# Eight input norms of a two-block transformer kernel: where the squares are kept and summed, one weight split, two rotary rotations

## The chip, the cores and the metric

One core of one Trainium2 chip runs the whole program. The metric is the device time in microseconds. Five engines matter: TensorE (PE in the profile; PEld is its weight load), VectorE (DVE), ScalarE (ACT), GpSimd (POOL) and SyncE (SP), which starts the weight transfers.

## The reference, cut to what matters

The program computes two blocks of depth 2 on 512 tokens of width 1024, in float32. The change touches the second one, and the norm on the border to it:

```
h = layer_norm(DEEPNORM_ALPHA * h + ff, ln2_g[l], ln2_b[l])      # end of the first block

for i in range(2):                                                # second block
    h = h + 0.5 * rms_norm(swiglu(rms_norm(h, g[0]), ...), g[1])
    hn = rms_norm(h, g[2])
    y = dilated_mixer(hn, ...) if i == 0 else window_gqa_mixer(hn, ...)   # mixer A, mixer B
    h = h + rms_norm(y, g[3])
    h = h + 0.5 * rms_norm(swiglu(rms_norm(h, g[4]), ...), g[5])
    e = p[i] @ ple_proj[i]
    gate = sigmoid(rms_norm(h, g[6]) @ ple_gate[i])
    h = h + rms_norm(e * gate, g[7])
```

`rms_norm(x, g)` is `x * rsqrt(mean(x*x)) * g`. Both mixers rotate the first 16 of the 64 features of each head of q and k (`apply_rope`): a swapped copy of the features is multiplied by a sine table and added to the features times a cosine table.

## The kernel before, in words

Activations lie transposed: 1024 features are 8 chunks (`DC`) of 128 partitions with 512 tokens along the free dimension. Every large product is made in three matmuls of 128 x 128 x 512 per pair of weight block and chunk (`piece`, L877 to L879): float32 is split into a high and a low part, and high*high, high*low, low*high are added. A unit of weights is 128 x 1024, eight such blocks. SyncE fetches units in order into a ring of four (`raw`), plus one unit set apart at the start of a section. ScalarE makes the high part `wh` (L1581) and VectorE the low part `wl` (L2058), in the order written in their streams; a ring place becomes free when TensorE has finished the unit that held it. TensorE waits for a unit's low part (`split_done`) before it uses the unit. All five streams are written out in one fixed order; the mixers' order comes from the generators `plan_a` and `plan_b`.

An RMS norm ahead of a product is not applied to the input. The product starts on the input times the gain, and the factor `rs_in` is multiplied in when VectorE takes a finished tile out of its bank. There are eight such places: ahead of ffn2 four times (once on the border to the second block, where the input comes out of `layer_norm`; three times behind `residual`), ahead of mixer A, ahead of mixer B, and ahead of the gate product twice. At each of them:

- VectorE's `residual` runs over the chunks k: the low part of the input `low_part(k)` (L2127), the sum `add(k+1)` (L2150), the part `part(k+2)` (L2145), and from k = 1 on `add_square(k)` (L2136), which adds the square of chunk k to `acc`. ScalarE's `pre_chunk(k)` makes the high part of the input (L1638) and then the square (`square`, L1603) into `sq[k % 2]`; from the third chunk on it first waits until VectorE has read that buffer.
- TensorE takes the chunks as they come: `first_tiles` works on three output tiles abreast (L921, L922, L928), nine matmuls for a chunk, and on a fourth tile that trails two chunks behind (ahead of the gate: four chunks behind), three matmuls for a chunk.
- When the three tiles are finished, and three pieces (gate: five pieces) of the fourth are still to be made, TensorE waits for the squares' sum and multiplies it by a matrix of 1/1024 (`pre_sum`, L1048). ScalarE then splits the unit behind the first four (`begin`), makes `rs_in` from the sum (L1595, L1596), and VectorE, which has split the same unit, uses `rs_in`: directly on tiles (L2197, L2763), or, ahead of a mixer, on the cosine and sine tables (`trig`, L2581, L2582).

In the mixers a tile of q or k is then rotated. VectorE shuffles (L2590) and multiplies by the cosine (L2591), which frees the bank, and GpSimd's `rope` multiplies the shuffled copy by the sine (L810) and adds (L811). `roped` of tile k waits until the rotation of two tiles earlier is over, since the shuffled copies alternate between two buffers. Splits of weight units stand between the tiles in VectorE's stream. Mixer B's first tiles are k0, v0, q0, q1 and k1; TensorE makes its first attention scores after two blocks of the fifth tile, and ahead of them it runs 20 matmuls of a constant (`stay_awake_in_next(20)`, L973), each of which the profile counts as two.

Ahead of the gate, TensorE still makes the embedding products while the chunks arrive. Five units are needed for them and the first three gate tiles: the third gate tile's unit is split by VectorE in `emb_splits` after chunk 2, the fourth tile's after chunk 4. In the stream of TensorE `first_tiles(GATED, before=before)` puts seven constant matmuls ahead of the third tile.

Of the kernel before, what the change touches and what calls it, by code (L numbers as in the profile page):

```python
# [391 lines left out]
def build(nc, stream, x_t, p_t, small, vecs, tab1, tab_a, tab_b, consts, out):  # L392
    n_units = stream.shape[0]
    with ExitStack() as ctx:
# [178 lines left out]

        SQ_HOMES = {2: prod[0], 3: prod[1], 5: tmp[0], 6: tmp[1], 7: sq[1]}
# [81 lines left out]
        def _(pool):  # L656
# [167 lines left out]
            def ropes_b():  # L824
                c.start(banks_mixer)
                for stage, k in plan_b():
                    if stage == "unit" and k < len(B_TILES):
                        c.next_tile()
                        if B_TILES[k][0] != "v":
                            rope(b_home(k)[:, :], tbb[:, B_SIN:B_SIN + S])  # L830
                    elif stage == "part":
                        c.next_tile()
# [38 lines left out]
        def _(pe):  # L871
# [16 lines left out]
            def unit(dst, src, chunks, start, stop, ready=None):  # L888

                pe.wait_ge(split_done, c.at("unit") + 1)  # L890
                for j, kc in enumerate(chunks):
                    if ready is not None:
                        c.wait(ready)
                    mm = piece(dst, c.n.get("unit", 0), kc % 8 * P, src, kc, start and j == 0,
                               stop and j == len(chunks) - 1)
                mm.then_inc(unit_done, 1)
                c.tick("unit")

            def tile(src, spread=(range(8),), ready=None):

                dst = free_tile()
                for n, chunks in enumerate(spread):
                    unit(dst, src, chunks, n == 0, n == len(spread) - 1, ready=ready)
# [9 lines left out]
            def abreast(u, t, kc, width, summed=True):  # L913
# [18 lines left out]
                if kc == 7 and summed:  # L932
                    pre_sum()

            def first_tiles(order, summed=True, before=None):
# [3 lines left out]
                for t, kc in order:  # L939
# [5 lines left out]
                    if t < width:  # L945
                        abreast(u, t, kc, width, summed)
                        continue
# [274 lines left out]
            def dense_n(layer, n, order):  # L1222
# [11 lines left out]
                if n < len(order):  # L1234
                    abreast(unit0[0], m, j, 2 if layer else 1, summed=False)
                    return
# [34 lines left out]
            for layer in range(DEPTH):  # L1271
# [57 lines left out]
                for half in range(2):  # L1329
                    if half == 0:  # L1330
                        first_tiles(BY_THREE, summed=False)
# [21 lines left out]
            def dense(n, n_tiles, part, o, outs0):  # L1353
# [150 lines left out]
            def mixer_b():  # L1504
                unit0[0] = c.n["unit"]
                c.start(banks_mixer)
                for stage, k in plan_b():
# [15 lines left out]
            for layer in range(DEPTH):  # L1523
# [44 lines left out]
        def _(act):  # L1568
# [67 lines left out]
            def pre_chunk(g, k, ready):  # L1636
# [18 lines left out]
            def rms_pre(g, then=None):  # L1655

                for k in range(DC):
                    pre_chunk(g, k, h_ready)
# [49 lines left out]
            for layer in range(DEPTH):  # L1708
# [142 lines left out]
                for m in range(DC):  # L1851
# [9 lines left out]
                    if m == 4:  # L1861
                        for k in range(5):
# [5 lines left out]
                           None if layer == 0 else lambda k: pre_chunk(V_RMS, k, affine))  # L1868
# [180 lines left out]
        def _(dve):  # L2049
# [27 lines left out]
            def layer_norm(g, to_x, wide=False):  # L2077
# [22 lines left out]
                for k in range(DC):  # L2100
# [14 lines left out]
                    if not to_x:  # L2115
                        add_square(k)
                        if k + 3 < DC:
                            centre(k + 3)
                if wide:
# [20 lines left out]
            def residual(g, pre, then=None):  # L2140
# [14 lines left out]
                for k in range(DC):  # L2155
# [5 lines left out]
                    add_square(k)  # L2161
# [431 lines left out]

            def part_of(m, last):
# [108 lines left out]
            def mixer_b():  # L2703
                trig(tbb[:, B_COS:B_COS + S], tbb[:, B_SIN:B_SIN + S], rs_in[:, :])
                c.start(banks_mixer)
                for stage, k in plan_b():
                    if stage == "unit":
                        unit_over()
                        if k < len(B_TILES):
                            src = bank[c.peek()][:, :]  # L2710
                            if B_TILES[k][0] == "v":
                                free(dve.tensor_tensor(bvs[:, :], src, rs_in[:, :], ALU.mult))
                            else:
# [19 lines left out]
            for layer in range(DEPTH):  # L2733
# [12 lines left out]
                def emb_splits(k):  # L2746
                    if k in (2, 4):
# [206 lines left out]
```

## Time and profile before

| | us |
|---|---|
| median of 3 runs | 3413.58 (3413.32 to 3414.89) |
| the profiled execution's own time | 3413.37 |
| its span, first to last instruction | 3411.5 |
| TensorE busy | 3339.1 (98%) |
| VectorE busy | 1836.1 (54%) |
| ScalarE busy | 1241.5 (36%) |
| GpSimd busy | 342.4 (10%) |

The profile shows one execution. Its own time is 1.9 us more than its span, and 0.2 us below the median. Busy time of TensorE counts the constant matmuls as work. The granted TensorE clock was 0.997 on the mean.

### The profile page before, as it was taken

How to read it: one execution, taken by the hardware profiler on the slowest of the kernel's cores; microseconds unless marked ns; L12 is line 12 of the kernel's file. 1: busy time of each engine (PE TensorE's matmuls, PEld its weight loads, DVE VectorE, ACT ScalarE, POOL GpSimd, SP SyncE). 2: the span in 40 equal slices, each digit the busy share in tenths (PEclk: the TensorE clock that was granted, in tenths of full speed). 3: DMA queues.
4: the chain of work that ended last, by engine and by line, in shares of the span. 5: the costliest groups of instructions: out<-in, count | busy, mean ns of one | idle time of the engine just before them, and what ended most of it. 6: DMA issues, size and time to landing. Idle time of an engine off the chain costs nothing.

```text
span 3411.5 us, 43291 instructions
## 1 busy us (share of the span) xinstructions
PE 3339.1 (98%) x16950; PEld 2661.6 (78%) x16950; DVE 1836.1 (54%) x2932; ACT 1241.5 (36%) x1878; POOL 342.4 (10%) x244
## 2 busy tenths in 40 slices
PE   9999999999999999999999999999999999999998
PEld 6767888776688887888777778887788876788886
DVE  5766334567753446443566664435644357654436
ACT  3354223424442324322333343324422235532324
POOL 0310000213100020000132200000000012100001
PEclk9999999999999999999999999999999999999999
DMA  4102232321122222223322122232222321132232
GB/s 163 62 32 73 94 99 98 124 69 44 56 81 99 96 95 87 93 97 105 113 69 71 66 81 98 95 103 98 87 92 98 105 95 43 58 104 93 99 106 79
DMA packets 81434, 300.40 MB, mean 88 GB/s; under 512 B 9040, under 2 KB 9040, under 8 KB 80640
## 3 DMA queue, kind: packets, MB, share of 16 engines
q1 hardware_dynamic: 78624, 284.20, 24.9%
q0 software_dynamic: 1568, 11.98, 0.9%
q8 instruction: 106, 1.74, 0.2%
q10 hardware_dynamic: 1088, 2.10, 0.2%
q14 instruction: 48, 0.39, 0.0%
HBM read 296.14 MB, written 2.10 MB: 87 GB/s over the span
## 4 chain that ended last, share of the span: by engine, by line
PE 88%; DVE 6%; ACT 3%; issue 1%; POOL 1%; DMA 1%; ACTq 0%; DVEq 0%; POOLq 0%
PE bank L877 25%; PE bank L879 25%; PE bank L878 25%; PE bank L921 2%; PE bank L928 2%; PE bank L922 2%; DVE wl L2058 1%; ACT sc L1742 1%; PE bank L1431 1%; PE bank L1443 1%; PE bank L1191 1%; PE bank L1172 1%; ACT wh L1581 1%; PE bank L1486 1%; PE bank L1130 1%
## 5 line engine op out<-in xcount | busy, mean ns | idle before, releaser
L877 PE MATMUL bank<-x,wh 128*128 128x512 f32 x2632 | 1053.1, 400 | 16.9 <-DVE h L2502 5.7
L879 PE MATMUL bank<-x,wl 128*128 128x512 f32 x2632 | 1027.3, 390 | 0.0
L878 PE MATMUL bank<-x,wh 128*128 128x512 f32 x2632 | 1026.3, 390 | 0.0
L1581 ACT ACTIVATE wh<-raw 128x1024 fp32r<-128x1024 f32 x528 | 558.1, 1058 | 1155.8 <-PE bank L879 1086.5
L2058 DVE TENSOR_TENSOR wl<-raw,wh 128x1024 fp32r<-128x1024 f32 x528 | 677.9, 1285 | 548.5 <-ACT wh L1581 547.3
L877 PEld LDWEIGHTS bank<-x,wh 128*128 128x128 f32 x2632 | 494.8, 188 | 138.2 <-issue 30.2
L879 PEld LDWEIGHTS bank<-x,wl 128*128 128x128 f32 x2632 | 494.5, 188 | 105.0
L878 PEld LDWEIGHTS bank<-x,wh 128*128 128x128 f32 x2632 | 495.3, 188 | 98.0 <-issue 3.4
L877 PE MATMUL bank<-mid,wh 128*128 128x512 f32 x1216 | 474.9, 391 | 0.5 <-DVE wl L2058 0.5
L878 PE MATMUL bank<-mid,wh 128*128 128x512 f32 x1216 | 473.1, 389 | 0.0
L879 PE MATMUL bank<-mid,wl 128*128 128x512 f32 x1216 | 473.1, 389 | 0.0
L877 PEld LDWEIGHTS bank<-mid,wh 128*128 128x128 f32 x1216 | 228.2, 188 | 49.6 <-DVE wl L2058 1.4
L878 PEld LDWEIGHTS bank<-mid,wh 128*128 128x128 f32 x1216 | 228.2, 188 | 48.1 <-issue 1.0
L879 PEld LDWEIGHTS bank<-mid,wl 128*128 128x128 f32 x1216 | 228.2, 188 | 47.6
L2197 DVE TENSOR_TENSOR prod<-bank,rs_in 128x512 f32<-128x512 f32 x88 | 60.7, 690 | 232.6 <-PE bank L879 232.6
L2074 DVE TENSOR_TENSOR mid<-prod,mid 128x512 f32 (+1 forms) x152 | 104.8, 689 | 88.4 <-ACT mid L1882 85.6
L680 POOL TENSOR_TENSOR acc<-sq,sq 128x512 f32<-128x512 f32 x8 | 11.2, 1398 | 1291.3 <-ACT sq L1687 1291.3
L2514 DVE TENSOR_TENSOR prod<-tmp,bank 128x512 f32<-128x512 f32 x64 | 43.9, 687 | 142.7 <-ACT tmp L1832 142.7
L1882 ACT ACTIVATE mid<-prod 128x512 f32 (+1 forms) x88 | 55.6, 632 | 174.7 <-DVE prod L2562 174.7
L1832 ACT ACTIVATE tmp<-bank 128x512 f32<-128x512 f32 x64 | 38.1, 595 | 178.4 <-PE bank L879 178.4
L921 PE MATMUL bank<-x,wh 128*128 128x512 f32 x200 | 80.1, 401 | 14.7 <-ACT x L1704 6.8
L2197 DVE TENSOR_TENSOR tmp<-bank,rs_in 128x512 f32<-128x512 f32 x88 | 60.8, 691 | 59.6 <-PE bank L879 58.4
(342 smaller groups left out, 3348.1 us busy)
## 6 DMA issues: line engine op xcount, KB each, us to landing
raw<-stream SPq DMA_DIRECT2D x528, 512.0 KB, 3.3
raw_apart<-stream SPq DMA_DIRECT2D x10, 512.0 KB, 3.6
sm<-small POOLq DMA_DIRECT2D x2, 2144.0 KB, 10.2
tb<-tab POOLq DMA_DIRECT2D x2, 1728.0 KB, 14.4
h<-x_t ACTq DMA_DIRECT2D x4, 512.0 KB, 7.1
out_t<-h SPq DMA_DIRECT2D x8, 256.0 KB, 2.1
tba<-tab_a POOLq DMA_DIRECT2D x1, 1152.0 KB, 9.2
pf<-p_t POOLq DMA_DIRECT2D x2, 512.0 KB, 5.2
```

What stands on the lines that cost most here:

```text
L877: pe.matmul(dst, hi, src[:, kc, 0, :], start=start, stop=False)
L878: pe.matmul(dst, hi, src[:, kc, 1, :], start=False, stop=False)
L879: return pe.matmul(dst, lo, src[:, kc, 0, :], start=False, stop=stop)
L921: pe.matmul(dst, hi, x[:, kc, 0, :], start=kc == 0, stop=False)
L922: pe.matmul(dst, lo, x[:, kc, 0, :], start=False, stop=False)
L928: mm = pe.matmul(dst, hi, x[:, kc, 1, :], start=False, stop=kc == 7)
L1581: act.activation(high_of(n)[:, :], raw_of(n)[:, :], ACT.Copy).then_inc(hi_done, 1)
L1882: act.activation(mid[:, i * 2 + k, 0, :], prod[k][:, :], ACT.Copy).then_inc(mid_hi, 1)
L2058: dve.tensor_tensor(low_of(n)[:, :], raw_of(n)[:, :], high_of(n)[:, :].bitcast(F32), ALU.subtract).then_inc(split_done, 1)
L2074: dve.tensor_tensor(dst, src, hi.bitcast(F32), ALU.subtract).then_inc(done, 1)
L2197: free(dve.tensor_tensor(dst, bank[c.peek()][:, :], rs_in[:, :], ALU.mult))
L2514: free(dve.tensor_tensor(prod[k % 2][:, :], tmp[k % 2][:, :], b[:, :], ALU.mult))
```

## The change

- ScalarE writes the squares of a norm's input to eight homes of their own, the chunks of `y` (used up by then), and behind the layer norm to `sq`, `tmp` and the upper four chunks of `y`. It waits for no reader.
- VectorE adds nothing after chunks 1 to 3, one square each after chunks 4, 5 and 6, and four after chunk 7. Behind the layer norm, the additions also stand after `centre` and not before it.
- TensorE's `pre_sum` moves behind the remaining pieces of the fourth tile: in the mixers and at the gate directly behind `first_tiles`, in ffn2 two further pieces later, inside the fifth tile.
- At the gate, the third gate tile's unit is split after chunk 1 (was 2), and the seven constant matmuls ahead of that tile are gone.
- In mixer B, the rotations of k0 and q0 are made on VectorE alone (`roped_whole`: shuffle, cosine product, sine product, sum), and the constant matmuls ahead of the first scores are 13 (were 20).

```diff
+        LN_HOMES = [sq[0][:, :], sq[1][:, :], tmp[0][:, :], tmp[1][:, :]] + [y[:, k, :] for k in range(4, DC)]
@@ GpSimd, ropes_b
-                        if B_TILES[k][0] != "v":
+                        if B_TILES[k][0] != "v" and k < 3:
+                            c.tick("rope")
+                        elif B_TILES[k][0] != "v":
                             rope(b_home(k)[:, :], tbb[:, B_SIN:B_SIN + S])
@@ TensorE
+            def unit(dst, src, chunks, start, stop, ready=None, sums=None):
                 pe.wait_ge(split_done, c.at("unit") + 1)
                 for j, kc in enumerate(chunks):
+                    if j == sums:
+                        pre_sum()
...
@@ abreast
-                if kc == 7 and summed:
-                    pre_sum()
@@ ffn2
                 first_tiles(BY_THREE)
                 for k in range(4):
-                    tile(x)
+                    tile(x, sums=2 if k == 0 else None)
@@ dense (mixers)
+                if n == len(BY_THREE):
+                    pre_sum()
@@ mixer_b
-                            stay_awake_in_next(20)
+                            stay_awake_in_next(13)
@@ gate
-                def before(t):
-                    if t == 2:
-                        stay_awake(7)
-                    pe.wait_ge(emb_read, 8 * layer + 3 + t)
-
-                first_tiles(GATED, before=before)
+                first_tiles(GATED, before=lambda t: pe.wait_ge(emb_read, 8 * layer + 3 + t))
+                pre_sum()
@@ ScalarE, pre_chunk
-                square(k)
+                act.activation(home[:, :], h[:, k, :], ACT.Square).then_inc(sq_made, 1)
+                c.tick("sqm")
@@ VectorE
-            def add_square(k):
-                if k:
-                    both = 2 if k == 1 else 1
+            def add_squares(k, homes):
+                for m in {4: [1], 5: [2], 6: [3], 7: [4, 5, 6, 7]}.get(k, []):
+                    both = 2 if m == 1 else 1
                     c.wait(sq_made, both)
-                    dve.tensor_tensor(acc[:, :], sq[0][:, :] if k == 1 else acc[:, :], sq[k % 2][:, :],
+                    dve.tensor_tensor(acc[:, :], homes[0] if m == 1 else acc[:, :], homes[m],
                                       ALU.add).then_inc(sq_used, both)
                     c.wait(sq_used, both)
...
+            def roped_whole(dst, src):
+                k = c.n.get("roped", 0)
+                dve.wait_ge(rotated, k)
+                rt = prod[k % 2][:, :]
+                link(dve.stream_shuffle(rt, src, SWAP))
+                free(dve.tensor_tensor(dst, src, tbb[:, B_COS:B_COS + S], ALU.mult))
+                link(dve.tensor_tensor(rt, rt, tbb[:, B_SIN:B_SIN + S], ALU.mult))
+                settled()
+                dve.tensor_tensor(dst, dst, rt, ALU.add).then_inc(rotated, 1)
+                c.tick("roped")
...
                 def emb_splits(k):
-                    if k in (2, 4):
+                    if k in (1, 4):
                         c.wait(unit_done)
                         split()
```

## Rows read from the trace of the kernel before

**Rows 1.** The page, part 1: engine, busy us, share of the span, instructions.
```profile
PE 3339.1 (98%) x16950; PEld 2661.6 (78%) x16950; DVE 1836.1 (54%) x2932; ACT 1241.5 (36%) x1878; POOL 342.4 (10%) x244
```

**Rows 2.** Waits of TensorE: us in total, times, longest us.
```profile
PE bank L921 <- ACT x L1638: 4.6, 6, 1.1
PE bank L1486 <- DVE scb L2645: 2.9, 4, 2.1
```

**Rows 3.** Groups by line, TensorE: busy us, mean ns | idle us before them.
```profile
L1048 PE MATMUL bank<-acc,ones 128*128 128x512 f32 x16 | 8.2, 590 | 0.0
```

**Rows 4.** Timeline of VectorE, first gate: start us, us, what, [idle before <-releaser].
```profile
2351.56 0.69 DVE L2136 TENSOR_TENSOR acc<-sq,sq 128x512 f32<-128x512 f32 x1
...
2354.93 1.23 DVE L2058 TENSOR_TENSOR wl<-raw,wh 128x1024 fp32r<-128x1024 f32 x1
...
2361.38 1.23 DVE L2058 TENSOR_TENSOR wl<-raw,wh 128x1024 fp32r<-128x1024 f32 x1
```

**Rows 5.** Timeline of ScalarE, first gate.
```profile
2350.49 1.05 ACT L1581 ACTIVATE wh<-raw 128x1024 fp32r<-128x1024 f32 x1
...
2352.82 1.06 ACT L2008 ACTIVATE emb<-bank 128x512 f32<-128x512 f32 x2
```

**Rows 6.** Timeline of TensorE, first gate, ahead of the third tile.
```profile
2354.10 1.72 PE L973 MATMUL bank<-ident,ones 128*128 128x128 f32 x14
2356.30 0.47 PE L921 MATMUL bank<-x,wh 128*128 128x512 f32 x1 [0.48 <-DVE wl L2058]
```

**Rows 7.** Timeline of TensorE, first gate, ahead of the fifth tile.
```profile
2379.56 0.47 PE L877 MATMUL bank<-x,wh 128*128 128x512 f32 x1 [1.25 <-DVE wl L2058]
```

**Rows 8.** Timeline of TensorE, third ffn2: the norm's matmul, starts of tiles five and six.
```profile
2429.48 1.02 PE L1048 MATMUL bank<-acc,ones 128*128 128x512 f32 x2
...
2432.43 0.39 PE L877 MATMUL bank<-x,wh 128*128 128x512 f32 x1
...
2437.87 0.39 PE L877 MATMUL bank<-x,wh 128*128 128x512 f32 x1
```

**Rows 9.** Timeline of VectorE, third ffn2: the split ahead of the fifth tile.
```profile
2430.41 1.22 DVE L2058 TENSOR_TENSOR wl<-raw,wh 128x1024 fp32r<-128x1024 f32 x1 [2.07 <-ACT wh L1581]
```

**Rows 10.** Timeline of TensorE, mixer A: the norm's matmul, starts of tiles six and seven.
```profile
1686.30 1.02 PE L1048 MATMUL bank<-acc,ones 128*128 128x512 f32 x2
...
1694.81 0.47 PE L877 MATMUL bank<-x,wh 128*128 128x512 f32 x1
...
1702.29 0.47 PE L877 MATMUL bank<-x,wh 128*128 128x512 f32 x1 [1.75 <-DVE wl L2058]
```

**Rows 11.** Timeline of VectorE, mixer A: cosine table, splits for tiles six and seven.
```profile
1688.74 1.05 DVE L2581 TENSOR_TENSOR tba<-tba,rs_in 128x512 f32<-128x512 f32 x1 [0.28 <-ACT rs_in L1596]
...
1693.29 1.38 DVE L2058 TENSOR_TENSOR wl<-raw,wh 128x1024 fp32r<-128x1024 f32 x1
...
1699.81 2.33 DVE L2058 TENSOR_TENSOR wl<-raw,wh 128x1024 fp32r<-128x1024 f32 x1
```

**Rows 12.** Timeline of TensorE, mixer B: constant matmuls, first scores, first transposes of probabilities.
```profile
2802.49 4.62 PE L973 MATMUL bank<-ident,ones 128*128 128x128 f32 x40
2807.96 0.70 PE L1474 MATMUL bank<-bk,bq 64*128 64x256 f32 x4 [0.84 <-POOL bq L811]
...
2817.44 0.33 PE L1486 MATMUL bank<-ident,scb 128*128 128x128 f32 x1 [2.10 <-DVE scb L2645]
```

**Rows 13.** Timeline of VectorE, mixer B: k0's shuffle, a split, the first scores' masking.
```profile
2799.24 0.74 DVE L2590 STREAM_SHUFFLE prod<-bank 128x512 f32<-128x512 f32 x1
...
2801.06 2.02 DVE L2058 TENSOR_TENSOR wl<-raw,wh 128x1024 fp32r<-128x1024 f32 x1
...
2808.77 0.38 DVE L2695 COPY scb<-sink 128x2 f32<-128x2 f32 x1 [2.00 <-PE bank L1474]
```

**Rows 14.** Windows: stretch, its us, busy us of each engine (instructions), PEclk, DMA share, GB/s.
```profile
279.70:283.11 3.41, 1.57 (x7) 0.99 (x6) 3.38 (x4) 1.41 (x2) 1.59 (x2) 1.00 0.08 34
283.11:286.52 3.41, 3.41 (x10) 2.61 (x9) 2.73 (x4) 1.26 (x2) 2.14 (x2) 0.50 0.01 2
```

More of the change, by code:

```diff
@@ L886, in free_tile @@
                 return bank[b][:, :]
-            def unit(dst, src, chunks, start, stop, ready=None):
+            def unit(dst, src, chunks, start, stop, ready=None, sums=None):
                 pe.wait_ge(split_done, c.at("unit") + 1)
                 for j, kc in enumerate(chunks):
+                    if j == sums:
+                        pre_sum()
                     if ready is not None:
@@ L897, in unit, with tile @@
                 c.tick("unit")
-            def tile(src, spread=(range(8),), ready=None):
+            def tile(src, spread=(range(8),), ready=None, sums=None):
                 dst = free_tile()
                 for n, chunks in enumerate(spread):
-                    unit(dst, src, chunks, n == 0, n == len(spread) - 1, ready=ready)
+                    unit(dst, src, chunks, n == 0, n == len(spread) - 1, ready=ready, sums=sums)
             def tiles_of(n, src, spread=(range(8),), ready=None):
@@ L911, in tiles_of, with abreast @@
                         tile(src, spread)
-            def abreast(u, t, kc, width, summed=True):
+            def abreast(u, t, kc, width):
                 if t == 0:
@@ L931, in abreast, with first_tiles @@
                         c.tick("unit")
-                if kc == 7 and summed:
-                    pre_sum()
-            def first_tiles(order, summed=True, before=None):
+            def first_tiles(order, before=None):
                 u = c.n["unit"]
@@ L945, in first_tiles @@
                     if t < width:
-                        abreast(u, t, kc, width, summed)
+                        abreast(u, t, kc, width)
                         continue
@@ L1234, in dense_n @@
                 if n < len(order):
-                    abreast(unit0[0], m, j, 2 if layer else 1, summed=False)
+                    abreast(unit0[0], m, j, 2 if layer else 1)
                     return
@@ L1330, in _ @@
                     if half == 0:
-                        first_tiles(BY_THREE, summed=False)
+                        first_tiles(BY_THREE)
                         for k in range(4):
@@ L1634, in begin, with pre_chunk @@
                 c.tick("begun")
-            def pre_chunk(g, k, ready):
+            def pre_chunk(g, k, ready, home):
                 c.wait(ready)
                 act.activation(x[:, k, 0, :], h[:, k, :], ACT.Copy, scale=vec[:, g + k:g + k + 1]).then_inc(x_hi, 1)
-                square(k)
+                act.activation(home[:, :], h[:, k, :], ACT.Square).then_inc(sq_made, 1)
+                c.tick("sqm")
             def unit_over():
@@ L1657, in rms_pre @@
                 for k in range(DC):
-                    pre_chunk(g, k, h_ready)
+                    pre_chunk(g, k, h_ready, y[:, k, :])
                     if then is not None:
@@ L1867, in _ @@
                 layer_norm(V_LN + 32 * layer + 16, V_LN + 32 * layer + 24, layer == 0,
-                           None if layer == 0 else lambda k: pre_chunk(V_RMS, k, affine))
+                           None if layer == 0 else lambda k: pre_chunk(V_RMS, k, affine, LN_HOMES[k]))
             def ffn2(embed=False):
@@ L2115, in layer_norm @@
                     if not to_x:
-                        add_square(k)
                         if k + 3 < DC:
                             centre(k + 3)
+                        add_squares(k, LN_HOMES)
                 if wide:
@@ L2160, in residual @@
                         part(k + 2)
-                    add_square(k)
+                    add_squares(k, [y[:, m, :] for m in range(DC)])
                     if then is not None:
@@ L2712, in mixer_b @@
                                 free(dve.tensor_tensor(bvs[:, :], src, rs_in[:, :], ALU.mult))
+                            elif k < 3:
+                                roped_whole(b_home(k)[:, :], src)
                             else:
```

## The prediction

> **What bounds the kernel now.** I read the page first: TensorE is busy for 98% of the span, the next engine for 54% [rows 1]. So nothing that only makes VectorE or ScalarE shorter can be seen in the time; what counts is where TensorE stands idle or runs constants. The second view was the list of TensorE's waits. It is short. One entry that lies where this change works is mixer B's probabilities (L1486); of the chunks of a norm's input it names the high part (L1638), six times in all, which is the start of the first chunk, and never the low part L2127 [rows 2]. The third was the group of the norm's own matmul: 8 calls, counted as 16, with 0.0 us of idle time before them [rows 3]. The squares' sum is never late today. That is the main thing for the reader to see: the change takes work off the path to a matmul that nobody waits for, and then puts that matmul later. What hangs behind it (`rs_in`, the tables, the first tiles) comes later too, so the question is who has slack there. For that I went through the timelines of the eight norms.
>
> The pace of TensorE: 24 matmuls from 2432.43 to 2437.87 [rows 8], 0.227 us each, so a chunk of nine takes 2.04 us and, with the trailing tile's three, 2.72 us. One L2136 addition is 0.69 us [rows 4].
>
> **Squares in homes of their own, additions at the end.** Three additions (2.0 us of VectorE) go from chunks 1 to 3 to the end, where four stand in a row: about 2.9 us at 0.69 plus 0.03 for the wait between them. In today's third ffn2 the last one ends 2 us before VectorE's next split, which waits for ScalarE [rows 9]; with three more at the end and the earlier chunks shorter by as much, they still end before that split starts. I take 0. It would be a gain if TensorE were waiting for chunks behind the first, which the list of waits doesn't show [rows 2]; idle times too short for it, one matmul's 0.2 us at each of eight norms, are the lower bound, -1.6. If the additions delay the split by as much as one of them, it costs +0.7 at each of six norms, 4 us, the upper bound. The value is nearest the first row, since the wait of 2.07 us ahead of the split [rows 9] is larger than what moves.
>
> **The norm's matmul moved behind three pieces, ffn2.** In the third ffn2 it starts at 2429.48 and the fifth tile at 2432.43 [rows 8]: nine matmuls are 2.04 us of that, the norm's matmul costs 0.91. Without it the fifth tile would start at 2431.52, but its unit's low part ends at 2430.41 + 1.22 = 2431.63 [rows 9], and TensorE resumes 0.15 us after such an end (the split of 1699.81 + 2.33 and the start at 1702.29 [rows 10, 11]): 2431.78. So 0.26 us of idle time appears that the norm's matmul covers today. The 0.91 is then paid inside the tile. Four such places: +1.0 us. `rs_in` is 3.4 us later there; the first bank that needs it is wanted by the sixth tile at 2437.87, and is free by about 2436. That cover holds, with 1.8 us to spare.
>
> **The same in mixer A.** Here the cover is missing. The norm's matmul goes from 1686.30 [rows 10] to 1688.34 + 0.26 = 1688.60, and all that VectorE does behind it moves by 2.3 us: the tables at 1688.74, two rotations, and only then the low part for the sixth tile, 1693.29 to 1694.67 [rows 11]. TensorE starts that tile at 1694.81 today, 0.14 us behind the split: no slack. It will start at 1697.1, after 2.1 us idle. The seventh tile waits 1.75 us today for the split at 1699.81 [rows 10, 11], in the same chain of VectorE and GpSimd; it moves by 2.3 us too. Those are one delay and not two: +2.3 us. Lower end 0 (if VectorE's order left slack that I don't see), upper end 2.3 plus one more wait of GpSimd's addition, about 1.3.
>
> **The same in mixer B, with two whole rotations on VectorE and seven fewer constants.** Twenty constants take 4.62 us, counted x40 [rows 12], so thirteen take 3.0. Today TensorE waits 0.84 us more behind them for GpSimd's second rotation, until 2807.96. In the new order k0 starts at 2799.24 + 2.30 = 2801.54 [rows 13]. A whole rotation occupies VectorE for a shuffle with its wait 0.79, cosine 0.61, sine with its wait 0.73 and sum 0.61: 2.74 us, against 1.24 today. These two operations are not in VectorE's rows; I price them as additions of the same shape [rows 4], bounds 0.6 and 1.3 each. Then v0 0.60, a split and q0: the split takes 2.02 us today, beside GpSimd's two operations [rows 13], and I take 1.2, as others do [rows 4], since GpSimd has nothing to do there any more. q0 is rotated at 2808.85, the scores start at 2808.9: +0.95. TensorE idles 2.8 us ahead of them, so the missing constants bring nothing by themselves.
>
> The Trainium skill, SBUF — State Buffer, section "Who interferes with whom", says that a VectorE instruction with two SBUF inputs and a GpSimd instruction that reads SBUF exclude each other for their whole length. The 2.02 us agrees with it. Without the rule, with 2.02 kept, the sum would be 0.8 us longer.
>
> After q0 come q1 (1.24) and the split behind it (1.2), and only then the masking of the first scores: 2811.2 in place of 2808.77, where VectorE today idles 2.00 us for TensorE [rows 13]. That idle time is used up. Behind it the order is as before, less a wait of 0.5 us for ScalarE: the transposes that start at 2817.44 [rows 12] start at 2819.3, +1.85 us, and TensorE idles 3.1 us ahead of them instead of 2.10. Bounds: +0.9 (only the scores' delay is kept) and +3.5 (sine and sum at 1.3 each, and the split contended).
>
> **The gate's third split.** The third tile waits for the low part made from 2354.93 to 2356.16 [rows 4]; until then TensorE runs seven constants for 1.72 us and idles 0.48 [rows 6]. The high part has been there since 2351.54 [rows 5], so behind chunk 1, where the addition of 2351.56 falls away, VectorE can split from 2351.6 to 2352.8. The bank is read out by the first of two copies from 2352.82 [rows 5], in the new order slightly earlier: free at 2353.4. TensorE can go on at 2354.10, where the constants stood: -2.20 us at each of two gates, -4.4. Chunk 2's low part then comes at 2353.5 and is wanted after 2357. The fourth tile's split is at 2361.38 today [rows 4] and will be near 2361; the tile is wanted at 2363.5. The norm's matmul moves behind 15 matmuls but is still ahead of the wait of 1.25 us for the fifth tile [rows 7], which hangs on a transfer started by the finished first tile and doesn't change. Bounds: -4.8 and 0.
>
> **Sum.** -4.4 + 1.0 + 2.3 + 1.85 = +0.8. From the profiled execution's 3413.37 (span 3411.5, 1.9 around it) that is 3414.1; the median shown is 0.2 higher, so 3414.4. What a measurement of this kernel can tell from no change is about 0.2%, 6.8 us: this is no change.
>
> **Rivals.**
>
> 1. *The clock gives way in the mixers (slower).* With 1.57 us of work in 3.41 us, 1.84 idle in one piece, the granted clock was 0.50 in the stretch that followed, the lower of its two levels, 1.2 GHz [rows 14]; behind 1.75 [rows 10] and 2.10 us idle [rows 12] it stayed up. I forecast idle times of 2.1 and 2.0 (mixer A), 2.8 and 3.1 us (mixer B). A stretch of 3.41 us at half clock is 1.7 us of work lost. Behind the first of each pair that is hidden in the second wait; behind the second nothing hides it: 1.7 in each mixer, 3417.8. [...] For it: the missing seven constants lengthen the idle piece. Against it: 2.10 us did nothing. 0.25.
> 2. *The mixers absorb the delay (faster).* If the tables were ready sooner than I derive, or the low parts are reordered in effect by ScalarE's earlier squares, the gates' gain stands alone: -4.4 + 1.0, 3410.2. Against it is the split that is waited for to 0.14 us today [rows 10, 11]. 0.22.
> 3. *The gate's change doesn't do what it says.* If the bank or the high part is late behind chunk 1, TensorE idles where it ran constants and only the costs are left: +0.8 + 4.4, 3418.8. The high part ends 0.05 us before VectorE wants it [rows 4, 5], but the tile is wanted 1.3 us after that. 0.07.
>
> The forecast has 0.46.
>
> **How the numbers follow.** All four cases lie within 0.2% of the time before. Rival 2 with the chunks' whole 1.6 us is 3408.6, the end of what I can add up on the fast side; rivals 1 and 3 together would be 3422. The range 3409.3 to 3418.9 leaves about one in ten out at either end together. Faster than 0.2% (under 3406.8) needs more idle time than these places have: 0.04. Slower than 0.2% (over 3420.4) needs rivals 1 and 3 together, or the upper ends of both mixers with rival 1: 0.07. No change: 0.89.
>
> **What would show it.** Gate: no L973 ahead of the third tile, which follows the second within 0.3 us; if L973's place is filled by an idle time, rival 3. ffn2: an idle time of about 0.1 to 0.3 us ahead of the fifth tile, L1048 six matmuls later. Mixer A: idle times of about 2 us ahead of both the sixth and the seventh tile, released by wl L2058; one of them missing would make the step wrong. Mixer B: about 2.8 us ahead of the first scores, released by a VectorE sum, about 3 us ahead of the first transposes. PEclk at 0.50 in either mixer would be rival 1. Additions that end later than ScalarE's high part behind the first tiles, or an idle time before L1048, would upset the first step.

## The result, and the profile after

| us | before | after |
|---|---|---|
| median of 11 runs beside each other | 3413.60 (3411.93 to 3415.61) | 3422.32 (3420.82 to 3424.64) |
| ratio of the times | | 1.0026 [1.0018, 1.0033] |
| the profiled execution, own time / span | 3413.37 / 3411.5 | 3423.08 / 3421.2 |

The change costs 8.7 us, 0.26%. The forecast was 3414.4, no change; the time lies above the forecast's range (3409.3 to 3418.9), and above the 0.2% that the prediction took as the border between slower and no change.

The page after, part 1, answers to [rows 1]: TensorE's busy share is the same and 42 instructions (the constants) are gone.

```profile
PE 3340.6 (98%) x16908; PEld 2658.1 (78%) x16908; DVE 1840.2 (54%) x2936; ACT 1240.0 (36%) x1878; POOL 336.4 (10%) x240
```

The waits of TensorE after (us in total, times, longest us), beside [rows 2]. L880 is the L877 of before.

```profile
PE bank L880 <- DVE wl L2059: 13.1, 10, 2.0
...
PE bank L926 <- ACT x L1638: 4.6, 6, 1.1
...
PE bank L1479 <- DVE bq L2605: 2.6, 1, 2.6
...
PE bank L1491 <- DVE scb L2659: 2.3, 4, 1.5
```

and the one row of before that answers to the first:

```profile
PE bank L877 <- DVE wl L2058: 5.9, 6, 1.8
```

Waits for a weight unit's low part have gone from six to ten and from 5.9 to 13.1 us. Five are new: one of 1.56 us in each ffn2, and one of 2.01 us in mixer A. One of 1.25 us at the start of the program is put down to another releaser in this list. The first experiment takes the four of ffn2 away again. The chunks' entry (L1638) is unchanged to the tenth, and the idle time before the norm's matmul is 0.1 us at all eight places together, where it was 0.0 (groups by line, as [rows 3]):

```profile
L1051 PE MATMUL bank<-acc,ones 128*128 128x512 f32 x16 | 8.3, 602 | 0.1
```

TensorE runs the same 12720 weight matmuls in the same order in both kernels. So one can lay the two timelines beside each other, matmul by matmul, and read how far each part of the program has slipped. That table, in us, is the backbone of what follows. It compares one profiled execution with one other:

| part | forecast | profiled pair |
|---|---|---|
| first block, not touched | 0 | +1.04 |
| ffn2, four times | +0.26 each | +2.27, +2.28, +2.28, +2.28 |
| mixer A | +2.3 | +2.31 |
| mixer B | +1.85 | +1.88 |
| gate, twice | -2.2 each | -2.29, -2.29 |
| sum | +0.8 | +9.8 |

The first block's +1.04 is, on balance, one more stretch of 3.4 us at half clock, near 930 us in this execution; the medians differ by 8.7. What the forecast missed stands in one row of the table, the ffn2's: 8.1 us. The row of mixer B needs care. Three more kernels below have the same mixer B, and the profile of each shows its own number, by where and for how long the granted clock fell: +1.9, +3.1 and +4.5.

**Third ffn2.** TensorE after, tile five, the norm's matmul, tile six. Beside it [rows 8].

```profile
2437.25 0.47 PE L880 MATMUL bank<-x,wh 128*128 128x512 f32 x1
...
2438.72 1.02 PE L1051 MATMUL bank<-acc,ones 128*128 128x512 f32 x2
...
2445.42 0.47 PE L880 MATMUL bank<-x,wh 128*128 128x512 f32 x1 [1.56 <-DVE wl L2059]
```

In [rows 8] the sixth tile has no idle time before it. Now it has 1.56 us, and not for a bank: for `wl`, the low part of its own weights. VectorE and ScalarE after, in the same place:

```profile
2435.88 1.23 DVE L2059 TENSOR_TENSOR wl<-raw,wh 128x1024 fp32r<-128x1024 f32 x1 [1.36 <-ACT wh L1581]
2441.16 0.69 DVE L2199 TENSOR_TENSOR tmp<-bank,rs_in 128x512 f32<-128x512 f32 x1 [4.05 <-ACT rs_in L1596]
2441.76 0.68 DVE L2199 TENSOR_TENSOR prod<-bank,rs_in 128x512 f32<-128x512 f32 x1
2444.05 1.23 DVE L2059 TENSOR_TENSOR wl<-raw,wh 128x1024 fp32r<-128x1024 f32 x1 [1.60 <-ACT wh L1581]
```

```profile
2439.77 0.69 ACT L1595 ACTIVATE rs_in<-bank,eps 128x512 f32<-128x512 f32 x1 [4.02 <-PE bank L1051]
2440.49 0.63 ACT L1596 ACTIVATE rs_in<-rs_in 128x512 f32<-128x512 f32 x1
2441.14 1.28 ACT L1878 ACT_TABLE_LOAD   x1
2442.43 0.63 ACT L1878 ACTIVATE tmp<-tmp 128x512 f32<-128x512 f32 x1
2442.97 1.04 ACT L1581 ACTIVATE wh<-raw 128x1024 fp32r<-128x1024 f32 x1
```

Before, the last two of these steps were (ScalarE, then VectorE):

```profile
2433.74 1.04 ACT L1581 ACTIVATE wh<-raw 128x1024 fp32r<-128x1024 f32 x1
```

```profile
2434.82 1.23 DVE L2058 TENSOR_TENSOR wl<-raw,wh 128x1024 fp32r<-128x1024 f32 x1 [1.60 <-ACT wh L1581]
```

Read ScalarE from top to bottom: the logarithm of the mean square, `rs_in` made from it, a table load, the activation of the scaled tile, and only then the high part of the sixth tile's unit. That unit needs nothing of the norm. ScalarE stands 4.02 us and VectorE 4.05 us in front of `rs_in` with its split behind them in the same streams. Before, the low part ended at 2434.82 + 1.23 = 2436.05, 1.82 us ahead of the tile, of which 0.15 is TensorE's resuming: 1.67 us of slack. In the kernel after, it ends at 2445.28, which is 9.23 later; the fifth tile starts 4.82 later; relative to it the split has moved by 4.41. The fifth tile itself is longer by the norm's matmul and a slower restart, 1.0. So 4.41 - 1.67 - 1.0 = 1.74 us are missing, and the start at 2445.42 comes 1.95 behind the last matmul at 2443.47 (one takes 0.23), 1.72 idle. That the two agree checks the bookkeeping only, since both come from this trace. From rows of before alone, `rs_in` 3.4 us later (the prediction's figure) less 1.67 us of slack is 1.7 us, an estimate that could have been made ahead. The fifth tile's own 0.26 (2437.25 against 2436.76 + 0.23) is exactly as forecast. The rest of the 2.28 is the first matmul behind each idle time, 0.31 in place of 0.23, and a little ahead of the seventh tile.

**Mixer A** is as forecast: idle times ahead of the sixth and the seventh tile, both released by the split, while [rows 10] has only the second.

```profile
1700.45 0.47 PE L880 MATMUL bank<-x,wh 128*128 128x512 f32 x1 [2.01 <-DVE wl L2059]
...
1707.90 0.47 PE L880 MATMUL bank<-x,wh 128*128 128x512 f32 x1 [1.75 <-DVE wl L2059]
```

**Mixer B.** VectorE after: the whole rotation of k0 and the split behind it, beside [rows 13]; then TensorE beside [rows 12].

```profile
2809.36 0.74 DVE L2601 STREAM_SHUFFLE prod<-bank 128x512 f32<-128x512 f32 x1
2810.14 0.69 DVE L2602 TENSOR_TENSOR bk<-bank,tbb 128x512 f32<-128x512 f32 x1
2810.74 0.68 DVE L2603 TENSOR_TENSOR prod<-prod,tbb 128x512 f32<-128x512 f32 x1
2811.46 0.69 DVE L2605 TENSOR_TENSOR bk<-bk,prod 128x512 f32<-128x512 f32 x1
...
2812.67 1.21 DVE L2059 TENSOR_TENSOR wl<-raw,wh 128x1024 fp32r<-128x1024 f32 x1
```

```profile
2816.63 0.49 PE L1479 MATMUL bank<-bk,bq 64*128 64x256 f32 x2 [2.58 <-DVE bq L2605]
...
2827.09 0.44 PE L1491 MATMUL bank<-ident,scb 128*128 128x128 f32 x2 [1.50 <-DVE scb L2659]
```

The rotation occupies VectorE for 2.71 us (priced 2.74), and the split takes 1.21 us, where it took 2.02 beside GpSimd's two operations. The second wait is 1.50 us and not the forecast 3.1, yet the sum is right. The windows (columns as in [rows 14]) say why:

```profile
2814.84:2818.25 3.41, 1.62 (x8) 1.15 (x9) 3.38 (x7) 0.00 (x0) 0.30 (x1) 1.00 0.01 2
2818.25:2821.66 3.41, 3.41 (x11) 1.72 (x10) 3.34 (x9) 1.38 (x2) 3.08 (x2) 0.50 0.35 108
```

Behind the idle time ahead of the scores the granted clock was 0.50 for one stretch, its lower level, 1.2 GHz; TensorE did its work there slower, arrived at the second wait later by that much, and found less of it. Where the clock held until then, in the run with three pieces below, the second wait was 3.07 us.

**Gate.** TensorE after, the end of the second tile's block and the start of the third's: nothing between them, where [rows 6] has 1.72 us of constants and 0.48 idle.

```profile
2361.71 0.39 PE L927 MATMUL bank<-x,wl 128*128 128x512 f32 x1
2361.93 0.39 PE L926 MATMUL bank<-x,wh 128*128 128x512 f32 x1
```

### The profile page after: what moved, and what is told of

Same layout as the page of the kernel before. It is cut to its first block, busy times and chain, and to the rows that moved or that the text cites. A ratio compares the mean times of both kernels' runs of the same rounds, so it can differ in the third digit from the quotient of the medians.

```text
span 3421.2 us, 43216 instructions
## 1 busy us (share of the span) xinstructions
PE 3340.6 (98%) x16908; PEld 2658.1 (78%) x16908; DVE 1840.2 (54%) x2936; ACT 1240.0 (36%) x1878; POOL 336.4 (10%) x240
## 3 DMA queue, kind: packets, MB, share of 16 engines
q8 instruction: 106, 1.74, 0.2%
## 4 chain that ended last, share of the span: by engine, by line
PE 88%; DVE 6%; ACT 3%; issue 2%; POOL 1%; DMA 0%; DVEq 0%; POOLq 0%; ACTq 0%
PE bank L880 25%; PE bank L882 25%; PE bank L881 25%; PE bank L926 2%; PE bank L927 2%; PE bank L933 2%; DVE wl L2059 1%; PE bank L1436 1%; ACT sc L1743 1%; PE bank L1448 1%; ACT wh L1581 1%; PE bank L1194 1%; PE bank L1175 1%; PE bank L1491 1%; PE bank L1133 1%
## 5 line engine op out<-in xcount | busy, mean ns | idle before, releaser
L880 PE MATMUL bank<-x,wh 128*128 128x512 f32 x2632 | 1053.4, 400 | 24.5 <-DVE wl L2059 12.6
L880 PEld LDWEIGHTS bank<-x,wh 128*128 128x128 f32 x2632 | 494.7, 188 | 149.5 <-issue 44.0
L880 PE MATMUL bank<-mid,wh 128*128 128x512 f32 x1216 | 474.9, 391 | 0.5 <-DVE wl L2059 0.5
L880 PEld LDWEIGHTS bank<-mid,wh 128*128 128x128 f32 x1216 | 228.3, 188 | 49.7 <-DVE wl L2059 1.3
```

Of the source, the lines that this page charges most:

```text
L880: pe.matmul(dst, hi, src[:, kc, 0, :], start=start, stop=False)
```

## The experiments

Theory 1 says that the ffn2's cost is the sixth tile's split behind a later `rs_in`. Theory 2 says that it is the additions at the end of the chunks, or the squares' new homes. Runs of one group share their runs of the kernel before, whose median was 3413.68 beside the first four, 3413.66 beside the others. Each kernel has 11 runs and one profile. Shifts are those of TensorE's weight matmuls against the profile of before. The ten kernels differ from before by less than 0.2%, so the places are told apart by the shifts.

**The norm's matmul of ffn2 back behind the three tiles abreast** (all else as after).

```diff
@@ first_tiles
+                        if summed and t == width - 1 and kc == 7:
+                            pre_sum()
@@ ffn2
-                first_tiles(BY_THREE)
+                first_tiles(BY_THREE, summed=True)
                 for k in range(4):
-                    tile(x, sums=2 if k == 0 else None)
+                    tile(x)
```

> The changed kernel with one part undone: in the four ffn2 the norm's matmul stands again directly behind the three tiles abreast; homes, additions at the end, gate, mixers stay changed. Theory 1 (queue): in ffn2 the low part of the sixth tile's unit stands behind rs_in in the streams of ScalarE and VectorE; rs_in 3.4 us later uses up the 1.8 us in which that low part was early, and TensorE idles 1.6 us ahead of the sixth tile and 0.1 ahead of the fifth, 2.28 us in each ffn2 by the shift of its matmuls. It expects -9.1 us against the changed kernel: 3413.2, no idle time ahead of the sixth tile. Theory 2 (additions): the four additions in a row, or the squares in y, hold up VectorE: 3422 stays, or TensorE now idles ahead of the norm's matmul (the last addition ends 0.4 us before that place).

Measured: 3413.39 (3411.05 to 3416.52), 0.9998 [0.9989, 1.0007]. The shift in every ffn2 is 0.0, with homes and late additions in place, and the waits for low parts fall back from 13.1 to 6.4:

```profile
PE bank L880 <- DVE wl L2061: 6.4, 6, 2.0
```

The 9 us are the place of this one matmul. Theory 2 falls. Mixer B, which is that of the kernel after, shows +3.1 here: the clock was 0.50 for 6.83 us behind a wait of 2.59 us ahead of the scores.

**The same in ffn2 and in the mixers.**

```diff
+                    if m == 2 and kc == 7:
+                        pre_sum()
-                if n == len(BY_THREE):
-                    pre_sum()
```

> As the kernel before this one, and the norm's matmul is also back at its old place in both mixers (the gates keep the new one). Theory 1: the mixers' shifts of +2.3 us (A) and +1.9 us (B) go as well: 3409.0, the sixth tile of mixer A starts without a wait of 2 us. Theory 2: if the whole rotations on VectorE are what costs in mixer B, only mixer A's 2.3 goes: 3411.

Measured: 3410.17 (3408.22 to 3412.21), 0.9988 [0.9979, 0.9997]. Mixer A's shift goes from +2.3 to 0.0, the gates keep -2.34 and -2.29. Mixer B still has +2.25, although its first transposes start 0.45 us earlier in the mixer than before: from 2814.69 on the granted clock was 0.50 for 6.83 us. The time lies between the 3409.0 and the 3411 expected and can't choose between the theories; the trace says that the delay of the transposes came from the moved matmul and that the clock then took the time anyway.

**The gate's change alone**, on the kernel before.

```diff
-                def before(t):
-                    if t == 2:
-                        stay_awake(7)
-                    pe.wait_ge(emb_read, 8 * layer + 3 + t)
-                first_tiles(GATED, before=before)
+                first_tiles(GATED, before=lambda t: pe.wait_ge(emb_read, 8 * layer + 3 + t))
@@ VectorE
-                    if k in (2, 4):
+                    if k in (1, 4):
```

> The kernel before with the gate's change alone: third tile's unit split behind chunk 1, the seven constant matmuls gone. Theory 1: -2.3 us at each of two gates, 3409.1 against 3413.6, the third tile starts directly behind the second. Rival: the gain needs the additions out of VectorE's way (here one of 0.69 us stands ahead of the split), and TensorE idles 0 to 0.5 us ahead of the third tile: 3410.

Measured: 3410.40 (3409.05 to 3411.55), 0.9990 [0.9981, 0.9999]. At the third tile the shifts are -2.29 and -2.30; with the wait for the fifth tile, which changes a little, they are -2.49 and -2.15. The median, 3.3 us faster, is nearer to the rival's 3410 than to 3409.1, but the rival's idle time isn't there. The third tile starts at the very time at which the constants did in [rows 6]:

```profile
2354.10 0.39 PE L921 MATMUL bank<-x,wh 128*128 128x512 f32 x1
```

**The two whole rotations and the 13 constants alone**, on the kernel before: the change's `roped_whole`, GpSimd's `ropes_b` for k < 3, and 20 to 13 in `stay_awake_in_next`.

```diff
+                            elif k < 3:
+                                roped_whole(b_home(k)[:, :], src)
-                            stay_awake_in_next(20)
+                            stay_awake_in_next(13)
```

> The kernel before with the two whole rotations on VectorE and 13 constant matmuls alone; the norm's matmul at its old place. Theory 1 (the delay of mixer B comes from the moved norm's matmul): the first scores start about 1.3 us earlier than before, the masking behind them at the same time, the first transposes 0 to 0.5 us earlier: 3413.2, no difference that can be measured. Rival (the rotations load VectorE too much): the first transposes come 1.5 to 2 us later: 3415.4.

Measured: 3415.64 (3411.90 to 3416.88), 1.0004 [0.9995, 1.0013]. TensorE after the constants:

```profile
2806.22 0.49 PE L1476 MATMUL bank<-bk,bq 64*128 64x256 f32 x2 [0.97 <-DVE bq L2605]
...
2816.66 0.47 PE L1488 MATMUL bank<-ident,scb 128*128 128x128 f32 x1 [3.08 <-DVE scb L2659]
```

and its windows:

```profile
2815.57:2818.98 3.41, 2.32 (x8) 2.03 (x9) 3.06 (x15) 2.48 (x8) 0.29 (x1) 0.50 0.01 2
2818.98:2822.40 3.42, 3.42 (x16) 1.76 (x14) 0.00 (x0) 0.62 (x3) 0.00 (x0) 0.50 0.00 0
```

The scores come at 2806.22 and not 2807.96 [rows 12], the transposes at 2816.66 and not 2817.44, so the rotations do what they are for. But TensorE reaches the transposes earlier still, idles 3.08 us in place of 2.10, and then works at half clock: the mixer ends 2.1 us later. The expectation of no difference missed the clock. The rival's 3415.4 came, but not by its mechanism, since the transposes aren't late. The interval of the times includes no change.

**The norm's matmul three pieces later in ffn2** (after has five): two pieces, 1.36 us, less delay.

```diff
-                    tile(x, sums=2 if k == 0 else None)
+                    tile(x, sums=0 if k == 0 else None)
```

> The changed kernel, the norm's matmul in ffn2 three pieces later than of old instead of five (ahead of the fifth tile's first block). Theory 1 (queue): rs_in comes 2.3 us later than of old in place of 3.65, the sixth tile's low part 0.5 to 0.7 us too late in place of 1.56 plus what the fifth tile loses; 0.6 to 0.9 us in each ffn2 instead of 2.28: about 3416.2. A rival in which the place itself costs (a float32 matmul between pieces, the weights' loads around it) expects no change from 3422.3.

Measured: 3416.85 (3414.66 to 3419.93), 1.0007 [0.9998, 1.0017]; shifts in ffn2 +0.84, +0.85, +0.81, +0.84. From the 1.74 missing above, 1.36 less leaves 0.38; with the fifth tile's 0.26 and two slow restarts that is 0.8. The price follows the delay beyond the slack, not the move as such. Mixer B, again that of the kernel after, shows +4.5: the clock held behind the first wait, and fell for 6.83 us behind the second.

```profile
2821.44 0.69 PE L1491 MATMUL bank<-ident,scb 128*128 128x128 f32 x2 [3.07 <-DVE scb L2659]
```

```profile
2820.52:2823.93 3.41, 2.49 (x8) 2.21 (x9) 2.92 (x13) 2.65 (x8) 0.12 (x1) 0.50 0.01 2
```

**The norm's matmul where after has it, the sixth tile's unit split ahead of `rs_in`** in ffn2.

```diff
@@ ScalarE
-            def pre_rstd():
+            def pre_rstd(early=0):
                 begin()
+                split(early)
@@ VectorE
-            def begin():
+            def begin(early=0):
                 c.wait(unit_done)
-                split()
+                split(1 + early)
@@ both, ffn2: no split behind the second tile
-                two(0, AFTER_NORM)
+                two(0, (0, 0, 0))
```

> The changed kernel with the norm's matmul left at its new place, but in ffn2 the sixth tile's unit is split ahead of rs_in on ScalarE and VectorE (its transfer has landed 1.8 us before the norm's matmul ends) and not behind the second tile. Theory 1 (the low part stands behind rs_in in the streams): the wait of 1.56 us ahead of the sixth tile goes, 0.3 to 0.7 us are left in each ffn2: 3415.5. Rival (late rs_in itself, by way of banks that are not free): the wait stays, released by a tile's reader and not by wl: 3422.3.

Measured: 3414.51 (3413.31 to 3417.24), 1.0003 [0.9994, 1.0012]; shifts +0.39, +0.39, +0.32, +0.39. VectorE, first ffn2, splits and then takes `rs_in`:

```profile
1324.44 1.23 DVE L2060 TENSOR_TENSOR wl<-raw,wh 128x1024 fp32r<-128x1024 f32 x1 [2.23 <-ACT wh L1581]
...
1326.26 0.69 DVE L2200 TENSOR_TENSOR tmp<-bank,rs_in 128x512 f32<-128x512 f32 x1 [0.60 <-ACT rs_in L1596]
```

This is the decisive run: counted from the start of this ffn2, VectorE takes the first tile with `rs_in` at the same time as in the kernel after, to 0.01 us, so that the banks come free no earlier, and 1.9 of the 2.28 us are gone. The bank was never the matter. What is left is nearly the forecast 0.26.

**Homes and additions alone**: after, with `pre_sum` at all eight norms, the gate's split and constants, and the rotations as before.

```diff
+        LN_HOMES = [sq[0][:, :], sq[1][:, :], tmp[0][:, :], tmp[1][:, :]] + [y[:, k, :] for k in range(4, DC)]
-                square(k)
+                act.activation(home[:, :], h[:, k, :], ACT.Square).then_inc(sq_made, 1)
+                c.tick("sqm")
```

> The kernel before with the squares' homes and the additions at the end alone; the norm's matmul at its old place everywhere, gate and rotations as before. Theory (no wait hung on the additions; the last one ends 0.4 us before the norm's matmul): TensorE's shift stays within 0.3 us at all eight norms, 3413.6. Rival (four additions in a row are late for the norm's matmul or for the next split): idle time ahead of L1048, up to 0.7 us at each of eight norms, 3416 to 3419.

Measured: 3412.20 (3410.32 to 3414.80), 0.9995 [0.9986, 1.0004]. The shift at the six norms of ffn2 and the mixers is 0.0 (mixer B's later loss to the clock is told in the last section); at the gates it is -0.68 and -0.69. The median is 1.5 us lower than before, about as much as the two together. The trace shows where it comes from: without the additions of chunks 1 and 2 ahead of it, VectorE starts the third gate tile's split 0.8 us earlier than in [rows 4] (the whole trace is 0.6 us early there), and the 0.48 us of idle time behind the constants in [rows 6] are gone.

```profile
2353.50 1.22 DVE L2063 TENSOR_TENSOR wl<-raw,wh 128x1024 fp32r<-128x1024 f32 x1
```

```profile
2354.95 0.48 PE L924 MATMUL bank<-x,wh 128*128 128x512 f32 x1
```

In the kernel after this adds nothing: with the split behind chunk 1 the gates have -2.29 with the homes and without them. The interval can't tell the sum of the two from nothing.

**Rotations with all 20 constants.** As the fourth kernel, but `stay_awake_in_next(20)`.

```diff
-                            stay_awake_in_next(13)
+                            stay_awake_in_next(20)
```

> The kernel before with the two whole rotations alone, and 20 constant matmuls as before (the run with 13 measured 3415.6; TensorE idled 0.97 and 3.08 us, the granted clock was 0.50 for 6.8 us from 2815.6 on, and its matmuls shifted by +2.2 us). Clock theory: the seven constants lengthened the idle piece ahead of the first transposes to 3.08 us; with 20 of them it is about 2.0, the clock stays up, and the shift of -0.35 at the transposes is all that is left: 3413.3. Rival (the loss comes from VectorE's order): 3415.6 again.

Measured: 3413.30 (3412.46 to 3415.18), 0.9998 [0.9989, 1.0007]. TensorE waits 2.54 us ahead of the transposes, and the clock still fell, for one stretch and not two:

```profile
2816.79 0.39 PE L1488 MATMUL bank<-ident,scb 128*128 128x128 f32 x1 [2.54 <-DVE scb L2659]
```

```profile
2816.93:2820.34 3.41, 3.41 (x12) 2.37 (x11) 1.91 (x8) 2.22 (x7) 0.00 (x0) 0.50 0.03 7
```

Mixer B ends 1.1 us late in place of 2.1. The time is as expected, the clock only half so. Of the 11 times, 3 are over 3414.5; with 13 constants 9 were. That is in favour of the clock theory, but the two kernels were not run beside each other, and each has one profile.

**Gate's change, and in mixer A the seventh tile's unit split one place later.** On the kernel before.

```diff
-                            split_after(k, AFTER_NORM)
+                            split_after(k, (0, 1, 1, 0))
```

> The kernel before with the gate's change (alone it measured 3410.4), and in mixer A the seventh tile's unit split by VectorE behind the third rotation instead of the fourth. Theory 1 (what TensorE waits for at these places is a split's position in VectorE's stream): the wait of 1.75 us ahead of the seventh tile goes: 3408.7. Rival (GpSimd and VectorE block each other there, so the split only gets longer or the scores come later): 3410.4.

Measured: 3408.56 (3408.16 to 3411.66), 0.9985 [0.9976, 0.9994]. The time came, the mechanism didn't: mixer A gains only 0.15 us. Its wait of 1.75 us [rows 10] has become two others:

```profile
1707.06 0.50 PE L877 MATMUL bank<-x,wh 128*128 128x512 f32 x1 [1.06 <-DVE aq L2586]
...
1712.92 0.70 PE L1417 MATMUL bank<-aq 64*128 64x512 f32 x2 [1.02 <-POOL aq L811]
```

3408.56 and the 3410.40 of the gate's change alone are within their scatter of each other; nothing shows a gain from this order.

**The repaired version**: the kernel after with the norm's matmul back in ffn2 and the mixers, 20 constants, and the order of the run above in mixer A.

```diff
+                        if summed and t == width - 1 and kc == 7:
+                            pre_sum()
-                    tile(x, sums=2 if k == 0 else None)
+                    tile(x)
-                if n == len(BY_THREE):
-                    pre_sum()
-                            stay_awake_in_next(13)
+                            stay_awake_in_next(20)
-                            split_after(k, AFTER_NORM)
+                            split_after(k, (0, 1, 1, 0))
```

> The changed kernel with the norm's matmul at its old place in ffn2 and the mixers, 20 constant matmuls in mixer B and mixer A's seventh unit split behind the third rotation. If homes and whole rotations bring nothing of their own, it equals the kernel with the gate's change and that split's place, 3408.6; the trace of that one shows that the split's place took away the wait of 1.75 us but left 1.06 us for a bank and 1.02 us for a rotation, so nearly all of the gain is the gates' 2.3 us each. If the homes spare something, it is below that by up to 1.6 us; if the whole rotations with their idle time ahead of the transposes cost clock, above it by 1 to 2 us: 3409.6 to 3410.6.

Measured: 3408.45 (3407.18 to 3410.69), 0.9984 [0.9975, 0.9993]. It is faster than both kernels, by 5.2 us than before and some 14 than after. The gates have -2.35 and -2.29, mixer B -0.45 with its clock up, behind the same wait of 2.54 us behind which it fell in the run with all 20 constants:

```profile
2813.72 0.55 PE L1493 MATMUL bank<-ident,scb 128*128 128x128 f32 x3 [2.54 <-DVE scb L2661]
```

```profile
2813.82:2817.23 3.41, 3.41 (x26) 2.37 (x26) 2.13 (x10) 2.37 (x7) 0.00 (x0) 1.00 0.01 2
```

The time is the same as that of the run before it, so nearly all of the gain is the gates'.

## Why the prediction was wrong, and where it was right

- **The failed step** is that of ffn2: "the first bank that needs it is wanted by the sixth tile at 2437.87, and is free by about 2436. That cover holds, with 1.8 us to spare." I followed `rs_in` to the data that need it, the bank, and not to what merely stands behind it in the two streams: the sixth tile's split, whose low part ended at 2436.05. I had just used such a split for the fifth tile, and in mixer A I did walk VectorE's stream on to the sixth; in ffn2 I stopped short of it. The term was taken as +0.26 four times and measured +2.28 four times. With the norm's matmul back it is 0.0, with two pieces less delay 0.84, with the split ahead 0.32 to 0.39. The prediction's own 3.4 us for `rs_in`, less 1.67 us of slack at the split, gives 1.7 us of idle time; 1.72 was measured.
- **Fifth tile, +0.26**: right to the hundredth, in the row at 2437.25.
- **Mixer A, +2.3**: measured +2.31, as one delay in two places, and 0.0 with the matmul back.
- **Mixer B, +1.85**: measured +1.88, in part by luck. The derivation held: counted from the mixer's start, the transposes come 1.86 us later, and the prices of the whole rotation and of the uncontended split were right. But three more profiles of the same mixer B have +1.9, +3.1 and +4.5, by where the clock fell; in this one the loss lay where the next wait hid it. The two dear ones are of executions 1.5 and 1.9 us above the median of their kernels. The four medians, less the shifts of the other places, leave 1.6 to 2.1 us for mixer B, an estimate within the scatter of the runs. The Trainium skill, SBUF — State Buffer, section "Who interferes with whom", says that a VectorE instruction with two inputs in SBUF contends with a GpSimd instruction that reads SBUF. The trace agrees: the split took 2.02 us beside GpSimd's two operations and 1.21 with GpSimd idle. Keeping 2.02 would have given +2.65.
- **Gates, -2.2 each**: measured -2.29 and -2.29 at the third tile, -2.29 and -2.30 with the gate's change alone. The fifth tile's waits are 1.24 and 1.33 us, where they were 1.25 and 1.18: nearly unchanged, as forecast. Rival 3 fell.
- **Homes and additions, 0**: 0.0 at six norms. By themselves they bring 0.7 us at each gate, which the forecast didn't see; in the kernel after that is part of the gates' -2.29.
- **Rival 1**, the clock, came true by half. In mixer B the clock fell behind 2.58 us idle ahead of the scores, and in this profile cost nothing, because the next wait was longer ("behind the first of each pair that is hidden in the second wait"). Behind the second waits it stayed up, in both mixers of this profile, so the 3.4 us were not paid. Behind mixer B's second wait that was the luck of the execution: with the same mixer B, the run with three pieces paid 2.6 us there, more than the 1.7 priced.
- **Rival 2** fell: the mixers absorbed nothing of what I had derived.
- **The range** held the sum's known terms and both of their bounds, but none for ffn2's second cover, since I had written it down as certain. With the measured 9.1 in that term and my own numbers in the others, -4.4 + 9.1 + 2.3 + 1.85 is +8.9; the medians differ by 8.7. The prediction names 3422 too, for rivals 1 and 3 together; that this is the time measured is chance, since neither is its cause.

## What to carry to other kernels

When a result is made later, follow the engines that wait for it, not only the data that need it: each instruction queued behind the first wait comes later too, and here a weight split, which needs nothing of the result, was the first to hurt. If such a wait must move, move the independent work ahead of it: that brought back 1.9 of 2.3 us a place here. Before constants ahead of such a wait are cut, look at the granted clock behind the longer idle time: in the profile with 13 constants it took back more than the earlier start had brought. And take no shift of one profile as the price of a place where TensorE idles for 2 us and more, before other executions have been looked at: one mixer B showed +1.9 to +4.5.

## What the runs showed of the hardware that was not expected

The granted clock doesn't go by the length of one idle time alone. It was at half in a stretch behind 1.84 us [rows 14], 2.54, 2.58 and 3.08 us idle; it stayed up behind 1.75 and 2.10 [rows 10, 12]; and with homes and additions alone, where mixer B is as before, it fell around a wait of 2.06 us there and the mixer ended 1.4 us later. Nor does it go by the order of the work: behind the wait of 2.54 us it fell in one kernel and held in another with the same work there; behind that of 2.58 or 2.59 it fell in three of four, for 3.41 us twice and 6.83 us once; behind mixer A's 2.01 us it fell in one of four. What decides it, these runs don't settle. A stretch of 3.41 us at half clock does at most 1.7 us less of work, and that costs time only as far as no wait behind it hides it: with the split ahead of `rs_in`, mixer A had one ahead of its sixth tile and was 3.91 us late there, and came out of its next wait 2.28 late, like the kernel after.

```profile
1697.37:1700.78 3.41, 3.41 (x9) 2.67 (x10) 1.32 (x3) 0.00 (x0) 3.33 (x3) 0.50 0.13 52
```
